# The first mixer of a two-block model: X ahead on the load queue, low parts of the weights on GpSimd, fewer filter taps on TensorE, branch a's norm under branch b's share of the output projection

## What is computed

```python
def conv_mixer(x, w_in, a_dw, a_dw_b, a_ln_g, a_ln_b, b_dw, w_out):
    u = jnp.einsum("bsd,de->bse", x, w_in)
    a_val, a_gate, b_b, b_c, b_x = jnp.split(
        u, [D_A, 2 * D_A, 2 * D_A + D_B, 2 * D_A + 2 * D_B], axis=-1)
    a = a_val * jax.nn.sigmoid(a_gate)
    a = causal_depthwise_conv(a, a_dw) + a_dw_b          # 31 taps
    a = jax.nn.silu(layer_norm(a, a_ln_g, a_ln_b))
    bb = b_b * causal_depthwise_conv(b_c * b_x, b_dw)    # 3 taps
    return jnp.einsum("bse,ed->bsd", jnp.concatenate([a, bb], axis=-1), w_out)
```

## Time and profile before

| | |
|---|---|
| median of three runs | 1865.53 us (1862.76 to 1869.09) |
| the profiled execution | 1861.7 us |
| its span, first to last instruction | 1860.4 us |
| PE busy | 1710.4 us, 92% |
| DVE busy | 796.0 us, 43% |
| ACT busy | 611.4 us, 33% |
| POOL busy | 121.3 us, 7% |
| loaded | 544.87 MB, mean 293 GB/s |
| mean granted TensorE clock | 0.983 |

### The profile page before, as it was taken

How to read it: one execution, slowest core, us unless ns; L and a number is a source line. 1 busy time by engine, 2 the same in 40 slices (tenths; PEclk the granted TensorE clock), 3 DMA queues, 4 the chain that set the end, 5 groups by cost and what they waited for, 6 DMA issues and landing times.

```text
span 1860.4 us, 23739 instructions
## 1 busy us (share of the span) xinstructions
PE 1710.4 (92%) x9910; PEld 1113.5 (60%) x9910; DVE 796.0 (43%) x1526; ACT 611.4 (33%) x1159; POOL 121.3 (7%) x141
## 2 busy tenths in 40 slices
PE   7978999998887987999998988699999999999998
PEld 7964443333232974344432322587999789779986
DVE  4952111111002774111110010566788667758885
ACT  4531010000001561011000001366666554646664
POOL 0000000000000000000000000033111000501110
PEclk9989999999999999999999999899999999999999
DMA  9439999999999639999999999443455544335550
GB/s 397 181 146 366 420 419 420 420 420 421 419 420 418 231 146 408 421 419 420 420 419 421 420 419 419 157 140 136 155 184 183 181 159 159 133 125 184 182 181 24
DMA packets 75362, 544.87 MB, mean 293 GB/s; under 512 B 8433, under 2 KB 8433, under 8 KB 9457
## 3 DMA queue, kind: packets, MB, share of 16 engines
q1 hardware_dynamic: 74304, 540.05, 73.0%
q10 hardware_dynamic: 944, 3.22, 0.4%
HBM read 542.19 MB, written 1.05 MB: 292 GB/s over the span
## 4 chain that ended last, share of the span: by engine, by line
PE 67%; DMA 21%; DVE 6%; ACT 3%; issue 1%; POOL 1%; SPq 0%; DVEq 0%; ACTq 0%
PE PS L897 21%; DMA ring<-in_w 16%; PE PS L342 12%; PE PS L344 12%; PE PS L343 12%; DMA F<-in_w 5%; PE PS L874 2%; PE PS L909 2%; PE PS L655 1%; DVE wl L325 1%; POOL sm L437 1%; DMA X<-in_x 1%; DVE X L547 1%; ACT wh L319 1%; PE PS L492 0%
## 5 line engine op out<-in xcount | busy, mean ns | idle before, releaser
L897 PE MATMUL PS<-ring,F 128*64 128x512 f32 x2112 | 477.7, 597 | 45.7 <-DMA ring<-in_w 41.3
L325 DVE TENSOR_TENSOR wl<-ring,wh 128x512 fp32r<-128x512 f32 x512 | 367.9, 739 | 187.2 <-ACT wh L319 184.2
L319 ACT ACTIVATE wh<-ring 128x512 fp32r<-128x512 f32 x512 | 319.4, 631 | 295.0 <-PE PS L344 291.4
L897 PEld LDWEIGHTS PS<-ring,F 128*64 128x64 f32 x2112 | 144.1, 136 | 362.7 <-issue 269.1
L342 PE MATMUL PS<-xh,wl 128*128 128x256 f32 x1216 | 351.5, 289 | 6.9 <-DVE xl L1547 2.1
L343 PE MATMUL PS<-xl,wh 128*128 128x256 f32 x1216 | 344.7, 283 | 0.0
L344 PE MATMUL PS<-xh,wh 128*128 128x256 f32 x1216 | 344.6, 283 | 0.0
L342 PEld LDWEIGHTS PS<-xh,wl 128*128 128x128 f32 x1216 | 233.9, 192 | 11.4 <-issue 5.8
L343 PEld LDWEIGHTS PS<-xl,wh 128*128 128x128 f32 x1216 | 234.1, 192 | 0.6
L344 PEld LDWEIGHTS PS<-xh,wh 128*128 128x128 f32 x1216 | 233.9, 192 | 0.0
L342 PE MATMUL PS<-wh,xl 128*128 128x512 f32 x368 | 149.0, 405 | 12.0 <-DVE wl L325 4.8
(11 more groups left out here) (332 smaller groups left out, 1746.7 us busy)
## 6 DMA issues: line engine op xcount, KB each, us to landing
ring<-in_w SPq DMA_DIRECT2D x264, 1024.0 KB, 26.5
F<-in_w SPq DMA_DIRECT2D x60, 1024.0 KB, 25.2
ring<-in_ffn_up SPq DMA_DIRECT2D x44, 1024.0 KB, 4.9
early<-in_w SPq DMA_DIRECT2D x40, 1024.0 KB, 26.2
ring<-in_ffn_down SPq DMA_DIRECT2D x22, 1024.0 KB, 4.9
ring<-in_even_w_in SPq DMA_DIRECT2D x10, 1024.0 KB, 18.3
Z<-in_w SPq DMA_DIRECT2D x10, 1024.0 KB, 24.5
XT<-in_w SPq DMA_DIRECT2D x10, 1024.0 KB, 25.3
```

Source lines behind the costliest of these rows:

```text
L319: act.e.activation(self.wh[:, p % NPIECE, :], self.piece_source(p), ACT.Copy).then_inc(*self.up("w_hi", p))
L325: dve.e.tensor_tensor(self.wl[:, p % NPIECE, :], self.piece_source(p), f32(self.wh[:, p % NPIECE, :]), ALU.subtract).then_inc(*self.up("w_ ...
L897: t = pe.e.matmul(PS[64 * half:64 * half + 64, bank, :], lhs(k), weights[:, a:a + 512], start=(k == 0), stop=(k == 7))
```

## The change

PE_TAPS goes from 12 to 6, so that DVE does 25 taps of each block of channels and PE 6, one behind each piece of chunks 3 to 8; ACT makes 24 diagonals instead of 48, one behind each piece from chunk 2 on. X is loaded in two halves by SP ahead of the weights, and ACT issues its three other loads behind its first four splits. The low parts of 40 of the 56 pieces of this stage (all of w_in but the first eight, and the first eight of w_out) are made by POOL in its own order; DVE makes the other 16. The chunks of w_in come in the order gate, value, gate, value, c, x, c, x, b, b. DVE's order is written out as one list. The first part of the projection's operand gets tiles of its own in F (early_gh, early_gl), so that it can be split while xh and xl are in use. The sums go ahead of the mean as before, but PE now does two pieces of q = 1 between mean and variance, and two between variance and spread, and the scaling comes in two halves; tanh applies gain and bias itself.

```diff
-PE_TAPS = 12
+PE_TAPS = 6
+POOL_PIECES = {*range(PIECES["ew_in"] + 8, PIECES["ew_in"] + 40), *range(PIECES["ew_out"], PIECES["ew_out"] + 8)}
...
+        self.left["ew_out", 0] = [nc.alloc_sbuf_tensor_at(n, [128, 2, T], F32R, offset=f_at + 4 * a)[:, :, :]
+                                  for n, a in (("early_gh", 6496), ("early_gl", 7008))]
...
-        order = {"ew_in": [2, 3, 0, 1, 6, 7, 8, 9, 4, 5], "ew_out": [2, 3, 0, 1],
+        order = {"ew_in": [2, 0, 3, 1, 6, 8, 7, 9, 4, 5], "ew_out": [2, 3, 0, 1],
...
+    def pool_split(self, p):
+        pool = self.pool
+        pool.wait_ge(self.at("w_hi", p))
+        pool.e.tensor_tensor(self.wl[:, p % NPIECE, :], self.piece_source(p), f32(self.wh[:, p % NPIECE, :]),
+                             ALU.subtract).then_inc(*self.up("w_lo_pool", p))
...
     def scalar_setup(self):
-        e.dma_start(self.X[:, :, :], A["x"].rearrange("(h p) d -> p h d", p=128)).then_inc(self.s_x, 16)
...
+    def sync_setup(self):
+        for h in range(2):
+            self.sp.e.dma_start(self.X[:, h, :], self.A["x"][h * 128:h * 128 + 128, :]).then_inc(self.x_in[h][0], 16)
...
     def even_tensor(self):
...
-                for _ in range(2 if c >= 4 else 0):
+                if 3 <= c < 9:
                     ch, k = conv // PE_TAPS, conv % PE_TAPS
-                    pe.wait_ge(at("ev_dve", 2 + ch // 2), at("ev_diag", conv), at("ev_pad"))
+                    pe.wait_ge(at("ev_dve", 1 + 2 * (ch // 2)), at("ev_diag", conv), at("ev_pad"))
...
+        for n in self.tensor_out("ew_out", p, 8, 1):
+            if n == p + 5:
+                pe.wait_ge(at("ev_square"))
+                for h in range(2):
+                    for c in range(4):
+                        t = pe.e.matmul(PS[:, 7, h:h + 1], v["sq"][:, c, h * 128:h * 128 + 128], self.mean512[:, 0:1],
+                                        start=(c == 0), stop=(c == 3))
+                t.then_inc(*up("ev_var"))
         pe.wait_ge(at("ev_rdiag", 1), at("consts", "ones"))
...
     def even_scalar(self):
         for n in range(NPIECE):
             self.scalar_split(n)
+        self.scalar_setup()
...
-                if c == 3 and j == 0:
+                if (c, j) == (2, 0):
                     act.wait_ge(self.cols_in, at("consts", "ident"))
...
-                for ch in {(8, 0): (0, 1), (8, 1): (2,), (8, 2): (3,)}.get((c, j), ()):
-                    act.wait_ge(at("ev_dve", 6 + ch // 2), at("ev_pad"))
+                for ch in {(6, 2): (0, 1), (8, 1): (2,), (8, 2): (3,)}.get((c, j), ()):
+                    act.wait_ge(at("ev_dve", 5 + 2 * (ch // 2)), at("ev_pad"))
                     act.e.activation(v["bacc"][:, ch, :], v["bP"][:, ch, 0:256], ACT.Copy,
                                      scale=v["bw"][:, ch, 0:1]).then_inc(*up("ev_btap", ch))
+                if (c, j) == (9, 1):
+                    self.scalar_split_x("ew_out", 0, self.GT[:, 0:2, :], at("ev_dve", 8))
...
-        for c in range(4):
-            act.wait_ge(at("ev_affine", c), at("ev_var"))
-            act.e.activation(v["sq"][:, c, :], v["acc"][:, c, :], ACT.Tanh).then_inc(*up("ev_tanh", c))
+        for h in range(2):
+            for c in (2 * h, 2 * h + 1):
+                act.wait_ge(at("ev_scaled", h), at("ev_var"), at("ev_consts", "bh"))
+                act.e.activation(v["sq"][:, c, :], v["acc"][:, c, :], ACT.Tanh, scale=v["gh"][:, c:c + 1],
+                                 bias=v["bh"][:, c:c + 1]).then_inc(*up("ev_tanh", c))
+            self.scalar_split_x("ew_out", 2 + h, self.GT[:, 4 + 2 * h:6 + 2 * h, :], at("ev_gated", 2 * h + 1))
...
     def even_vector(self):
+        for n in range(NPIECE, 2 * NPIECE):
+            self.vector_split(n)
...
+        value(0)
+        convolve(22)
+        value(1)
+        convolve(30)
+        product(0)
+        convolve(20)
+        convolve_b(0)
+        convolve(6)
+        product(1)
+        convolve(6)
+        convolve_b(1)
+        convolve(4)
+        gate_b(0)
+        convolve(3)
+        self.vector_split_x("ew_out", 0, self.GT[:, 0:2, :])
+        convolve(5)
+        gate_b(1)
+        convolve(2)
+        self.vector_split_x("ew_out", 1, self.GT[:, 2:4, :])
+        convolve(len(taps))
...
     def even_pool(self):
+        for p in sorted(POOL_PIECES):
+            self.pool_split(p)
         for h in range(2):
             self.pool_rstd(h, ("ev", h))
```

More of the change, by code:

```diff
@@ L371, in tensor_columns @@
             h, l = self.weight(p + k)
-            pe.wait_ge(self.at("w_lo", p + k), self.at("x_lo", stage, k // 2))
+            pe.wait_ge(self.low(p + k), self.at("x_lo", stage, k // 2))
             for m in range(2):
@@ L381, in tensor_out @@
         pe, PS = self.pe, self.PS
+        xh, xl = self.operand(stage, q)
         pe.wait_ge(self.at("g_lo", stage, q))
@@ L416, in out_done, with operand @@
         return self.at("w_used", p + 2 * nk - 2 + d) if m else self.at("half_done", stage, d)
+    def operand(self, stage, q):
+        s = slice(2 * q % 8, 2 * q % 8 + 2)
+        return self.left.get((stage, q), (self.xh[:, s, :], self.xl[:, s, :]))
     def scalar_split_x(self, stage, q, src, *ready):
-        s = slice(2 * q % 8, 2 * q % 8 + 2)
         self.act.wait_ge(*ready)
-        self.act.e.activation(self.xh[:, s, :], src, ACT.Copy).then_inc(*self.up("g_hi", stage, q))
+        self.act.e.activation(self.operand(stage, q)[0], src, ACT.Copy).then_inc(*self.up("g_hi", stage, q))
     def vector_split_x(self, stage, q, src):
-        s = slice(2 * q % 8, 2 * q % 8 + 2)
+        xh, xl = self.operand(stage, q)
         self.dve.wait_ge(self.at("g_hi", stage, q))
-        self.dve.e.tensor_tensor(self.xl[:, s, :], src, f32(self.xh[:, s, :]), ALU.subtract).then_inc(
-            *self.up("g_lo", stage, q))
+        self.dve.e.tensor_tensor(xl, src, f32(xh), ALU.subtract).then_inc(*self.up("g_lo", stage, q))
     def vector_rstd(self, var, eps, h, key):
@@ L710, in even_scalar @@
-                for ch in {(8, 0): (0, 1), (8, 1): (2,), (8, 2): (3,)}.get((c, j), ()):
-                    act.wait_ge(at("ev_dve", 6 + ch // 2), at("ev_pad"))
+                if c >= 2 and diag < 4 * PE_TAPS:
+                    if diag >= 6:
+                        act.wait_ge(at("ev_conv", diag - 6))
+                    ch, k = diag // PE_TAPS, diag % PE_TAPS
+                    act.e.activation(v["dgs"][diag % 6], self.ident[:, :], ACT.Copy,
+                                     scale=v["aw"][:, ch, k:k + 1]).then_inc(*up("ev_diag", diag))
+                    diag += 1
@@ L754, in even_vector, with value @@
         dve.wait_ge(at("ev_pad"), at("ev_consts", "bh"))
+        p = PIECES["ew_in"]
         taps = [(k, c) for half in range(2) for k in range(PE_TAPS, 31) for c in (2 * half, 2 * half + 1)]
-        b_taps = [(k, c) for c in range(4) for k in range(3)]
+        def value(half):
+            c, i = 1 + 2 * half, 2 * half
+            dve.wait_ge(at("w_used", p + 4 * c + 3), at("ev_act", c - 1))
+            dve.e.scalar_tensor_tensor(out=aP[:, i:i + 2, 30:286], in0=v["sg"][:, i:i + 2, :], scalar=1.0,
+                                       in1=self.bank2(c), op0=ALU.add, op1=ALU.mult).then_inc(*up("ev_dve", c))
         def convolve(n):
@@ L769, in convolve, with product, convolve_b @@
                 t.then_inc(*up("ev_tap", c, k))
-        def convolve_b(n):
-            for _ in range(min(n, len(b_taps))):
-                k, c = b_taps.pop(0)
-                if k:
+        def product(half):
+            c, i = 5 + 2 * half, 2 * half
+            dve.wait_ge(at("w_used", p + 4 * c + 3), at("ev_act", c - 1))
+            dve.e.tensor_tensor(bP[:, i:i + 2, 2:258], v["bc"][:, i:i + 2, :], self.bank2((5, 1)[half]),
+                                ALU.mult).then_inc(*up("ev_dve", c))
+        def convolve_b(half):
+            for k in (1, 2):
+                for c in (2 * half, 2 * half + 1):
                     dve.wait_ge(at("ev_btap", c) if k == 1 else at("ev_btap2", c, 1))
```

150 lines of the change are left out of this document (62 added, 88 removed).

## The result

The changed kernel takes 1871.32 us (median of 19 runs, 1867.84 to 1877.93), the kernel before 1866.10 (19 runs, 1861.21 to 1870.40): ratio 1.0028, interval 1.0017 to 1.0039. So the change makes the kernel 0.28% slower, with 1 outside the interval. The forecast was 1872.7, the range 1847 to 1884. The profiled execution of after took 1873.9 us, 2.6 above its median, that of before 1861.7, 4.4 under its own; so the two profiles are 12.2 us apart, 7 more than the medians.

What follows compares the result with a forecast made beforehand. Expert loads, resuming after the projection's last piece, bound the kernel; DVE sets the last sum. 113.3 + 27.3 = 140.6 instead of 133.4 is 7.2 us later: 1872.7 us on the median of 1865.5, range 1847 to 1884.

Steps and rivals of the forecast that it cites:

- The price of a low part on POOL: First mixer, taps: each low part made by POOL beside DVE's taps stops DVE for 1.05 us.
- the upper bound: DVE's loss per low part on POOL, bounded by 0 and 1.05 us; the forecast took 1.05, full block, chance 0.47.
- The number of stops: Mixer up to the last sum: 37 blocks of DVE, 38.9 us, less about 3 us beside operations that read PSUM.
- DVE never idles: Mixer up to the last sum: DVE works or is blocked throughout, busy over 95% from 26 to 113 us.
- mere cover: Chunk 6: PE stands from about 64 to 73 us behind ACT's wait for DVE, without becoming the bound.
- the third rival: PE's stand costs by itself through its low clock, or POOL is blocked repeatedly: 4 to 10 us more, 1877 to 1884, chance 0.18.
- The last sum: End of the convolution sums on DVE: at 113.3 us, where it was 104.2.
- The first product: Start of the mixer on PE: with X loaded first, at 12.7 us instead of 15.15, a gain of 2.4.
- The tail: Last sum to the projection's last piece, with the norm between: 27.3 us, 1.9 less than before.
- a rival only: PE's lower clock on mean, variance and q=1 or chunk 9: 4 to 10 us more, part of a case with chance 0.18.
- the norm's part misjudged: Failure sign after the mixer's sums: last sum at 113 with the projection's last piece beyond 143 us.
- The norm's own gain: Norm with two q=1 pieces beside centring and two beside the powers: last sum to last piece 1.9 us shorter.

Runs made afterwards that it cites:

- e1: The changed kernel with all low parts back on DVE, DVE's list written anew and POOL idle: 1857.55 us, ratio to the kernel before 0.9961.
- e2: The changed kernel with POOL only writing zeros into the low parts, so part of the computation is left out: 1844.59 us, ratio to the kernel before 0.9886.
- e8: The all-low-parts-on-DVE variant of the changed kernel, with 20 low parts (every second chunk's) on POOL: 1865.52 us, ratio to the kernel before 0.9989.
- e10: The changed kernel with branch a's sums in PSUM, all 124 taps on DVE and none on PE: 1849.37 us, ratio to the kernel before 0.9912.
- e12: Control to e10: same order on every engine, but branch a's sums in SBUF: 1879.53 us, ratio to the kernel before 1.0064.
- e4: Probe without the model's work: streams of 24 DVE operations, each met by two POOL operations; a tap stream takes 9.59 us alone, two subtractions add 2.01.
- e3: The kernel before with X alone moved ahead of the weights on SP, ACT's three other loads left in place: 1866.40 us, ratio 1.0011.
- e11: The kernel before with X first, ACT's three loads behind its first splits, DVE's pieces 4 to 7 ahead of its wait for cols: 1867.09 us, ratio 0.9995.
- e6: The changed kernel with q=1 of the output projection back behind the spread: 1873.58 us, ratio to the kernel before 1.0047.

## Why the prediction was right, point by point

- **The price of a low part on POOL** was taken as 1.05 us; measured 1.02 to 1.04 in the kernel and 1.005 by itself. The choice of the upper bound, by the pairs of the earlier trace rows, was the step that carried the forecast, and e1, e2, e8 and the pair e10/e12 show it to be the cause. The rule of the Trainium skill (SBUF — State Buffer, "Who interferes with whom") agrees with these numbers for operations of DVE with two inputs in SBUF, and the variant with sums in PSUM uses it. For one input it says that there is no stop outside DVE's two-port modes; the one-input operation of e4 was stopped all the same, 1.35 to 1.44 us for 0.40, and no run shows in which mode it was.
- **The number of stops** was 37 less 3; 30 operations of DVE after the first value were in fact stopped (rows of over 1.2 us in the timeline), for 30.6 us instead of 35.9. The rest fell where DVE stood, beside operations that read PSUM, or into the stream that starved POOL.
- **"DVE never idles" failed.** It idled for 6.9 us (4.14, 2.14 and 0.66), and was busy for 91% of the time from 26 to 113 us, not for over 95%. The forecast had PE standing from about 64 to 73 as mere cover; PE stood from 66.2 to 80.9, since POOL was starved for 11.46 us on top of the wait that was foreseen, and so became the bound for a moment. The stand cost little in sum: four low parts, the held one and the three made while DVE stood, stopped nothing, 4.1 us at 1.03 each (an estimate), against the 4.14 of idling. This is one piece of the third rival (POOL held off by taps that follow closely), by a mechanism that it only touched.
- **The last sum** was put at 113.3 and ended at 112.33. That is right partly by cancelling: 5.3 us too much for stops, and DVE's own work 48.8 instead of 51.2 (79.35 busy less 30.6; a tap is 0.40 in a stream, not 0.42), against 6.9 of idling that was not in the sum.
- **The first product** came at 11.89, better than the 12.7 forecast, and the first value at 25.34 (25.6): of the additional 0.8 only 0.3 were left, since PE's clock was low in the first chunks (window mean 0.89). By e3 and e11 X first gives the kernel before no gain that can be measured.
- **The tail was mis-sized.** 27.3 us were forecast, 30.2 measured. The first row of it is the mean: PE had stood for 5.26 us before it, its clock was 0.50 of full speed in the window from 112 to 116, and DVE waited 3.94 us for it, where the sum had 2.0. That row is 1.9 of the 2.9 us. A second low stretch (0.50 from 128 to 133 us) fell on the pieces of q=2. Where PE was not starved (e2) the tail was 27.05, last sum to early loads, at a mean clock of 0.94 instead of 0.80. So the steps fit, and what the sum left out is the clock, which the forecast named in a rival only. The last piece ended at 142.97, at the edge of the 143 beyond which the forecast wanted to call the norm's part misjudged. The norm's own gain of 1.9 is not shown by e6.
- **The total.** The last matmul of the projection came 9.2 us later than before, not 7.2: the last sum 8.1 later where 9.1 was forecast, the tail 1.1 longer where it was to be 1.9 shorter. The medians moved by 5.2. That the time given is off by only 1.4 us is in part luck: counted in the two profiles, as the sum counts, the change costs 9.2, and it is the scatter of single executions (the profile of before was a quick one) that brings the medians down to 5.2, on the other side of 7.2.

## What to carry to other kernels

Work moved to POOL is not free for DVE when both read two operands from SBUF: price each POOL operation at the time for which it stops DVE (here 1.03 us lost for 0.61 saved), and look where the second operand lives before the work is moved. A sum that a long stream updates belongs in PSUM if two banks can be had; with all taps on DVE and the low parts on POOL it took this kernel from 1879.5 to 1849.4 us. Time won ahead of a stretch in which PE stands can be lost to its lower clock there, so look at the granted clock on both sides of the wait before a few microseconds are booked.

## What the runs showed of the hardware that was not expected

- A steady stream of DVE operations can hold one POOL operation off until the stream ends (11.46 us in two kernels, 7.1 to 8.4 us in 72 of 96 tries of a probe), where POOL's operation starts within some 0.1 us around the boundary of two of them; holds of 2.1 and 2.3 us were also seen at two other starts. In another probe this was 6 of 60, and at other starts 0 of 23. What tips it is open.
- An operation with a single tensor input in SBUF and its scalars in SBUF is stopped as well (1.35 to 1.44 us for 0.40), and a POOL operation with one input (0.69 to 0.80 us) costs a tap 0.35 us.
- Taps whose sum is read from and written to PSUM cost the same 0.40 us as those in SBUF.
- Of 3.2 us won at the first product 1.15 were left at the last sum, 90 us later, and none at the early loads: PE's granted clock from 12 to 26 us, 1.00 in the kernel before, was 0.79 when the products began early, behind a stand of 4.0 us.
